# One gate chunk as seven products of 2x2 blocks, in a fused decoder layer on one Trainium2 core

## What is computed

```python
h  = rms_norm(x, mix_norm)
z  = h @ w_in                                  # heads of four mixers, then gl: 4 x 1024 gate columns
o  = stack([o_a, o_b, o_c, o_d], axis=2)       # four branches, 256 wide each
proj = einsum('bsnw,nwd->bsnd', o, w_branch)
gate = sigmoid(gl).reshape(B, S, N_BRANCH, D_MODEL)
merged = sum(gate * proj, axis=2)
x = x + merged @ w_out
x = x + swiglu_ffn(rms_norm(x, ffn_norm), w_gate, w_up, w_down)
```

## Time and profile before

| | us |
|---|---|
| median of 3 runs | 755.29 (755.27 to 755.92) |
| the profiled execution, its own time | 754.7 |
| its span, first to last instruction | 752.9 |
| TensorE busy | 747.9 (99%) |
| VectorE busy | 592.7 (79%) |
| ScalarE busy | 404.8 (54%) |
| GpSimd busy | 104.9 (14%) |

### The profile page before, as it was taken

One profiled execution on the slowest core, in us unless ns is written; L12 is line 12 of the kernel. 1 busy time (PEld: TensorE's weight loads), 2 busy tenths in 40 slices (PEclk: granted clock), 3 DMA queues, 4 the chain that ended last, 5 costly groups with the idle time before them and its releaser, 6 DMA issues.

```text
span 752.9 us, 11500 instructions
## 1 busy us (share of the span) xinstructions
PE 747.9 (99%) x4506; PEld 660.9 (88%) x4506; DVE 592.7 (79%) x819; ACT 404.8 (54%) x629; POOL 104.9 (14%) x131
## 2 busy tenths in 40 slices
PE   8999999999999999999999999999999999999998
PEld 8988888888888888788888899999889999999887
DVE  6655988878788976425978989889989888888991
...
GB/s 292 96 239 56 57 58 112 82 87 57 57 111 112 57 93 75 112 57 279 85 93 169 185 113 167 114 111 199 5 260 110 109 110 109 113 113 328 66 26 84
DMA packets 67877, 89.55 MB, mean 119 GB/s; under 512 B 3108, under 2 KB 52592, under 8 KB 67696
## 3 DMA queue, kind: packets, MB, share of 16 engines
...
q0 software_dynamic: 1456, 3.09, 2.0%
...
## 4 chain that ended last, share of the span: by engine, by line
PE 99%; DVE 0%; issue 0%; POOL 0%; ACT 0%; POOLq 0%; DVEq 0%
PE bank L2365 15%; PE bank L2367 15%; PE bank L2366 15%; PE bank L2795 8%; PE bank L2794 8%; PE bank L2793 8%; PE bank L2874 5%; PE bank L2876 5%; PE bank L2878 5%; PE bank L2732 2%; PE bank L2733 2%; PE bank L2734 2%; PE bank L2764 1%; PE bank L2765 1%; PE bank L2763 1%; PE bank L2580 1%
## 5 line engine op out<-in xcount | busy, mean ns | idle before, releaser
L2365 PE MATMUL bank<-h_hi,w_hi 128*128 128x512 f32 (+1 forms) x352 | 134.7, 383 | 0.0
L2367 PE MATMUL bank<-h_hi,w_lo 128*128 128x512 f32 (+1 forms) x352 | 133.7, 380 | 0.0
L2366 PE MATMUL bank<-h_lo,w_hi 128*128 128x512 f32 (+1 forms) x352 | 133.6, 379 | 0.0
L2793 PE MATMUL bank<-t_hi,w_hi 128*128 128x256 f32 x320 | 88.4, 276 | 0.0
L2795 PE MATMUL bank<-t_hi,w_lo 128*128 128x256 f32 x320 | 88.3, 276 | 0.0
L2794 PE MATMUL bank<-t_lo,w_hi 128*128 128x256 f32 x320 | 88.3, 276 | 0.0
L1538 DVE TENSOR_TENSOR w_lo<-raw,w_hi 128x2048 fp32r<-128x2048 f32 x27 | 64.2, 2381 | 23.4 <-ACT w_hi L927 16.1
L2367 PEld LDWEIGHTS bank<-h_hi,w_lo 128*128 128x128 f32 x352 | 66.2, 188 | 12.7
L2365 PEld LDWEIGHTS bank<-h_hi,w_hi 128*128 128x128 f32 x352 | 66.2, 188 | 12.6 <-issue 0.3
L2366 PEld LDWEIGHTS bank<-h_lo,w_hi 128*128 128x128 f32 x352 | 66.2, 188 | 12.1
L2794 PE MATMUL bank<-f_lo,w_hi 128*128 128x256 f32 x240 | 66.3, 276 | 0.0
...
## 6 DMA issues: line engine op xcount, KB each, us to landing
...
```

Of the source, the lines that this page charges most:

```text
L2365: mm(dst, l_hi, r_hi, start=start, stop=False)
L2366: mm(dst, l_hi, r_lo, start=False, stop=False)
L2367: return mm(dst, l_lo, r_hi, start=False, stop=stop)
L2793: mm(dst, l_hi, r_hi, start=begin and k == 0, stop=False, skip_group_check=True)
```

## The change

The first of the last branch's four gate chunks, chunk 27, gets the kind "seven". It runs as seven block products with `wino_chunk`, 7 x 12 matmuls of 256 columns, in place of 48 matmuls of 512 columns. Its banks are 6 and 7 (the two gate tiles), 2 and 3.

- The sums of h: GpSimd adds high and low parts of four blocks of h back together (`whole_block`, eight instructions of 128x512, between its own adds of the third branch); VectorE makes T3, T1, T2, T4 from them (`gate_sums`, at the end of iteration 24), ScalarE their high parts (iteration 25), VectorE their low parts (`gate_lows`, iteration 25). They lie where the softmax attention's keys and probabilities were.
- The weight sums and low parts: VectorE, four instructions of 128x512 in iteration 24 and four for the low parts at the end of iteration 25; ScalarE four for the high parts, one before each of the first four tiles of chunk 26. The two half splits of chunk 27 fall away on ScalarE and the one split on VectorE.
- ScalarE and VectorE each get a `seven_products` in iteration 27. The two gate tiles are taken after the products: tile 1 after the sixth, tile 0 after the seventh, and in that order they go on to VectorE, GpSimd, `merged_high` and `merged_low`.
- ScalarE's high part of O11 moves from between the two sigmoids of chunk 27 to behind both of them and behind the first `merged_high`. It waits for all seven products as well, since `seven_lo` lies in that memory.
- `out_unit(0)` waits for at least two merged low parts.
- `weight_sums`, `weight_lows`, `wino_split` and `wino_chunk` are moved up in the program so that chunk 27 can call them; the feed-forward part calls them as before, its semaphore counts shifted.

The diff, cut:

```diff
+    SEVEN = MIXER_CHUNKS - D // CW
+    assert chunks[SEVEN][4] == ("gate", N_BRANCH - 1, 0)
+    chunks[SEVEN] = ("seven",) + chunks[SEVEN][1:]
+
+    def gate_tiles(c):
+
+        return (1, 0) if c == SEVEN else (0, 1)
...
+        SEVEN_LO = O11_AT + 3 * LINE // 8
+        seven_lo = place("seven_lo", [P, 7 * QUAD], F32R, at=SEVEN_LO)
+        seven_sum = place("seven_sum", [P, 7 * QUAD], at=SEVEN_LO)
...
+        g_hi = place("g_hi", [P, 4, KT // 2, SEQ // 2], F32R, at=MG0 + 16 * KB)
+        g_lo = place("g_lo", [P, 4, KT // 2, SEQ // 2], F32R, at=MG0)
+        g_sum = place("g_sum", [P, 4, KT // 2, SEQ // 2], at=MG0)
+        g_first = place("g_first", [P, KT // 2, SEQ // 2], at=MG0 + 16 * KB)
...
+        SEVEN_BANK = (bank[6], bank[7], bank[2], bank[3])
...
+            def whole_block(dst, ks, toks):
+
+                for half in range(2):
+                    part = slice(ks.start + 2 * half, ks.start + 2 * half + 2)
+                    ins = pool.tensor_tensor(dst[:, 2 * half:2 * half + 2, :], h_hi[:, part, toks].bitcast(F32),
+                                             h_lo[:, part, toks].bitcast(F32), ALU.add)
+                ins.then_inc(S["t_made"], 1)
+
+            T1, T2, T3, T4 = range(4)
             for m in range(1, N_BRANCH):
-                for d in range(KT):
-                    y = (m - 1) * KT + d
+                for n, d in enumerate(gate_tiles(SEVEN) + tuple(range(CT, KT)) if m == N_BRANCH - 1 else range(KT)):
+                    y = (m - 1) * KT + n
+                    if (m, d) == (N_BRANCH - 2, 4):
+                        pool.wait_ge(S["prob_turned"], HEADS * TT)
+                        whole_block(g_sum[:, T1], LOWER, T2ND)
+                        whole_block(g_sum[:, T2], UPPER, T2ND)
+                    elif (m, d) == (N_BRANCH - 2, 5):
+                        whole_block(g_first, LOWER, T1ST)
+                        whole_block(g_sum[:, T4], UPPER, T1ST)
                     pool.wait_ge(S["gated"], y + 1)
                     if m > 1:
-                        pool.wait_ge(S["proj_added"], y + 1 - KT)
+                        pool.wait_ge(S["proj_added"], (m - 2) * KT + d + 1)
                     pool.tensor_tensor(merged[:, d, :], merged[:, d, :], two[:, y % 2, :], ALU.add)\
                         .then_inc(S["proj_added"], 1)
 
...
-                if d == 0:
+                done = SEVEN_ORDER.index(d)
+                act.wait_ge(S["proj_added"], (N_BRANCH - 2) * KT + done + 1)
+                if done == 0:
                     act.wait_ge(S["attn_out"], 1)
...
                     act.wait_ge(S["o11_in"], 16)
+                    act.wait_ge(S["product_done"], 7)
...
+                    if c + 1 == SEVEN:
+                        if d < 4:
+                            wino_split(SEVEN, (0, 2, 3, 1)[d])
+                    elif d in halves_at:
...
+                    if j == 1 and c == SEVEN - 2:
+                        for i in (2, 0, 1, 3):
+                            act.wait_ge(S["t_made"], SEVEN_SUMS)
+                            nact.activation(g_hi[:, i], g_sum[:, i], ACT.Copy).then_inc(S["t_hi_ready"], 1)
...
+            def seven_products():
+
+                f0, f1, first, last = SEVEN_BANK
+                act.wait_ge(S["product_done"], 1)
+                nact.activation(f0[:, T1ST], first[:, T1ST], ACT.Copy).then_inc(S["c11_seeded"], 1)
+                act.wait_ge(S["product_done"], 2)
+                nact.activation(gate_seventh[:, :], last[:, T1ST], ACT.Copy).then_inc(S["seventh_copied"], 1)
+                act.wait_ge(S["product_done"], 5)
+                nact.activation(f0[:, T2ND], first[:, T1ST], ACT.Copy).then_inc(S["c12_seeded"], 1)
+                for n, j in enumerate(gate_tiles(SEVEN)):
+                    y = (N_BRANCH - 2) * KT + n
+                    if j == 1:
+                        act.wait_ge(S["product_done"], 6)
+                        act.wait_ge(S["c22_ready"], 1)
+                    else:
+                        act.wait_ge(S["product_done"], 7)
+                    act.wait_ge(S["proj_added"], y - 1)
+                    nact.activation(two[:, y % 2, :], SEVEN_BANK[j][:, :], ACT.Sigmoid).then_inc(S["gate_taken"], 1)
+                merged_high(SEVEN_ORDER[0])
+                out_high(O11)
 
...
+                elif c == SEVEN:
+                    seven_products()
...
+            def gate_sums():
+
+                T1, T2, T3, T4 = (g_sum[:, i] for i in range(4))
+                made = SEVEN_SUMS - 4
+                dve.wait_ge(S["t_made"], made)
+                vec.tensor_tensor(T3, T2, T1, ALU.subtract).then_inc(S["t_made"], 1)
+                dve.wait_ge(S["t_made"], made + 1)
+                vec.tensor_tensor(T1, T1, g_first[:, :, :], ALU.subtract).then_inc(S["t_made"], 1)
+                dve.wait_ge(S["t_made"], made + 2)
+                vec.tensor_tensor(T2, T2, T1, ALU.subtract).then_inc(S["t_made"], 1)
+                dve.wait_ge(S["t_made"], made + 3)
+                vec.tensor_tensor(T4, T4, T2, ALU.subtract).then_inc(S["t_made"], 1)
+
+            def gate_lows():
+
+                for n, i in enumerate((2, 0, 1, 3)):
+                    dve.wait_ge(S["t_hi_ready"], n + 1)
+                    vec.tensor_tensor(g_lo[:, i], g_sum[:, i], g_hi[:, i].bitcast(F32), ALU.subtract)\
+                        .then_inc(S["t_lo_ready"], 1)
+
+            def seven_products():
+
+                _, f1, first, _ = SEVEN_BANK
+                dve.wait_ge(S["product_done"], 3)
+                dve.wait_ge(S["seventh_copied"], 1)
+                vec.tensor_tensor(f1[:, T1ST], first[:, T1ST], gate_seventh[:, :], ALU.add).then_inc(S["c21_seeded"], 1)
+                dve.wait_ge(S["product_done"], 6)
+                dve.wait_ge(S["c12_seeded"], 1)
+                vec.tensor_tensor(f1[:, T2ND], first[:, T1ST], gate_seventh[:, :], ALU.add).then_inc(S["c22_ready"], 1)
+
             def gated(c):
 
...
                 _, m, q = chunks[c][4]
-                for j in range(CT):
+                for n, j in enumerate(gate_tiles(c)):
                     d = CT * q + j
-                    y = (m - 1) * KT + d
+                    y = (m - 1) * KT + CT * q + n
                     if q == 0:
                         wait_taken(dve, fill_at[PROJ_AT[m]] + d)
-                    wait_taken(dve, fill_at[c] + j)
+                    if c == SEVEN:
+                        dve.wait_ge(S["gate_taken"], n + 1)
+                    else:
+                        wait_taken(dve, fill_at[c] + j)
                     v = two[:, y % 2, :]
                     vec.tensor_tensor(v, v, branch[:, d, :], ALU.mult).then_inc(S["gated"], 1)
+                    if (c, j) == (SEVEN - 2, 0):
+                        gate_lows()
                     if m == N_BRANCH - 1:
-                        if d > 0:
-                            merged_low(d - 1)
-                        out_behind(d)
+                        if CT * q + n > 0:
+                            merged_low(SEVEN_ORDER[CT * q + n - 1])
+                        out_behind(CT * q + n)
 
             for c in range(MIXER_CHUNKS):
                 kind, _, _, _, what = chunks[c]
...
+                if c == SEVEN - 3:
+                    weight_sums(SEVEN)
+                    gate_sums()
+                elif c == SEVEN - 2:
+                    for step in (0, 2, 3, 1):
+                        weight_lows(SEVEN, step)
...
+                if c == SEVEN:
+                    wino_chunk(c)
                     continue
...
-                        pe.wait_ge(S["mg_lo_ready"], KT // 2 * n + k + 1)
+                        pe.wait_ge(S["mg_lo_ready"], max(KT // 2 * n + k + 1, CT))```

The places that the diff does not show by itself. VectorE around chunk 27, before: the rows from the first gate tile of the last branch to the low part of chunk 29's weights (`o_78`, `o_79`, `o_80` are `o11`, `o12`, `o22`; L1538 is `split`).

```order
L1538 TENSOR_TENSOR w_lo<-raw,w_hi 128x2048 [waits hi_ready] x2
L1913 TENSOR_TENSOR two<-two,branch 128x512 [waits taken1]
L1862 TENSOR_TENSOR o_lo<-o_78,o_hi 128x2048 [waits out_hi]
L1913 TENSOR_TENSOR two<-two,branch 128x512 [waits taken0]
L1855 TENSOR_TENSOR mg_lo<-merged,mg_hi 128x256 [waits mg_hi_ready]
L1867 TENSOR_TENSOR o_79<-o_79,o_78 128x2048 [waits out_t_made,right_half_in]
L1538 TENSOR_TENSOR w_lo<-raw,w_hi 128x2048 [waits hi_ready]
```

280 lines of the change are left out of this document (154 added, 126 removed).

## The result

The changed kernel takes 760.54 us (median of 17 runs, 759.87 to 761.28); the kernel before, beside it on the same chip, takes 755.42. The medians differ by 5.1 us, where 3.8 were forecast. The ratio is 1.0062, with a 95% interval of 1.0051 to 1.0072, which is 4.7 us, between 3.9 and 5.4. Now and then an execution takes some 5 us more than the others of its kernel (two of the 17 of before, 760.4 and 760.85; one of the ten of before beside e1 to e4; two of the twelve of e12), which moves a ratio more than a median. The profiled execution has a span of 758.1 us against 752.9, 5.2 more, with the granted clock of TensorE at 1.00.

A forecast was written before the change was run, and what follows sets the result against it. TensorE, busy 99% of the span, was taken as the bound, with VectorE's queue just under it. Terms -1.36 + 0.1 + 0.35 + 2.25 + 2.0 + 0.45 = +3.8 us gave 759.1 us, range 756.8 to 760.8.

The forecast's parts named there:

- the three late waits: TensorE waits forecast at the head of chunk 29 (2.25 us), in A12 (2.0) and in S2 (0.45).
- the forecast's own upper bound: Whole kernel: 760.0 us in the forecast's own case, if the handovers are longer.
- Chunk 27 is late: Rival, preparing chunk 27: GpSimd's sums slow VectorE, TensorE waits 1 to 3 us more, 761 us; chance 0.08.
- late gates: Chunk 27's gate tiles complete only at its end; VectorE starts O11's low part 5.0 us later.
- signs of being wrong: O11's low part before 355, VectorE idle in chunks 28 to 30, or TensorE waiting at the head of chunk 26 or 27.
- -1.36 forecast for the products: Chunk 27 on TensorE: 48 wide matmuls (10.88 us) replaced by 84 narrow ones (9.52 us), -1.36 us.
- narrow matmuls do not pay: Rival, chunk 27: each 256-column matmul is held to its 188 ns weight load, 760.2 us; chance 0.02.
- The first seed: Third product of chunk 27: ScalarE's seed copy stands behind chunk 28's split, TensorE waits 0.35 us.
- its 4.5 less 0.8: Chunk 29, A12 and S2: the three waits are VectorE's lateness of 4.5 less S2's slack of 0.8.
- only part lands: Rival: chunk 29's wait comes but VectorE makes up for it before the output units, +1.3 us, 756.6; chance 0.10.
- The saving reaches the end: Rival: VectorE's queue gives back 5.0 us or O11 comes by 353, so 753.9 us; chance 0.04.
- All this costs nothing: Preparing chunk 27, iterations 24 and 25: the extra sums and low parts cost zero, upper bound about 1 us.

The follow-up runs named there:

- e1: Kernel before, without seven products, only ScalarE's high part of O11 and its merged high part in chunk 27 as late as the change makes them; ratio to before 1.0047.
- e4: Changed kernel with VectorE's difference o12 - o11 ahead of O11's low part, its wait also counting O22's load; ratio to before 1.0082.
- e12: e10 with the block sums of h back on GpSimd; ratio to before 1.0015, 755.92 us against 755.54 of before.
- e10: Changed kernel with block sums and last branch's adds on VectorE, O11's high part between the sigmoids, chunk 28's weights behind the first seeds; 753.58 us, ratio to before 0.9978.
- e7: Changed kernel with block sums on VectorE, O11's high part between the sigmoids, last gate tile's multiplication first, chunk 28's weights behind the first seeds; ratio to before 1.0014.
- e3: Changed kernel with ScalarE's high part of O11 between the two sigmoids of chunk 27; ratio to before 1.0042.
- e11: Changed kernel with the difference o12 - o11 ahead of O11's low part, waiting for O12's load alone; ratio to before 1.0030.
- e5: Changed kernel with VectorE's multiplication of the last gate tile ahead of OT1's low part and the first two sums for S2; ratio to before 1.0059.
- e2: Changed kernel with the block sums of h made by VectorE as four 1024-column sums, none by GpSimd; ratio to before 1.0052.

## Why the prediction was right, and where it was off

The direction and the three late waits came as forecast, by the mechanism forecast. The number is in the range with some luck: 760.54 is above the forecast's own upper bound, 760.0, and just under the end of the range, 760.8, which had been put near the rival "Chunk 27 is late". What came is what that rival described, the late gates and a wait ahead of them, and one of the prediction's own signs of being wrong, a wait at the head of chunk 26, is there.

*TensorE.* -1.36 forecast for the products. From the head of chunk 27 to that of chunk 28 the time fell from 10.88 to 354.22 - 344.31 = 9.91, which with the wait at the third product is -0.97; forecast -1.01. The narrow matmuls keep their pace of 0.113 us. The rival "narrow matmuls do not pay" is refuted by this and by e10.

*The first seed.* 0.35 forecast, 0.25 measured, and by the cause named: e7 removes it by moving ScalarE's split behind the copy.

*Late gates.* Forecast 2.25 at chunk 29, 2.0 in A12, 0.45 in S2; measured 2.33, 1.73 and 0.32, and some 0.4 us beside them in the longer distances behind these waits. The three are one thing, as the prediction said (its 4.5 less 0.8 is not the sum of the three, which is 4.7, but near what is left of them beside the 1.0 that TensorE gains): e1 makes them without the seven products, and e3 and e11 take 2.2 and 2.4 us out of the sum by two different ways of letting VectorE begin sooner.

*VectorE regains nothing.* The rival "only part lands" asked for idle time in chunks 28 to 30. It is not there: from O11's low part at 358.62 to 395 VectorE stands idle once, for 0.91 us at 391.21, and e5 could gain 0.3 us only.

*The saving reaches the end.* It did not, by this change. e10 shows an arrangement in which it does: O11's low part at 355.00 with the head of chunk 25 at 321.36, which is 354.5 in before's time, and shorter instructions behind it.

*The step that failed: "All this costs nothing".* The preparation of chunk 27 was costed at zero with 1 us as the upper bound; it cost 1.26 us at the head of chunk 26, and e12 against e10 measures GpSimd's block sums alone at 1.27. The walk-through took the four weight sums at 685 ns from a row where GpSimd is idle, and put GpSimd's eight sums at 1.29 each from a row where VectorE is. Side by side they take 1.75 and up to 1.88. The four sums alone came 4 x 1.06 = 4.2 us later to their end, against a slack that the prediction itself had given as 2.8. The rival "Chunk 27 is late" had this mechanism, its row and even its place (chunk 26's weights past 331.88), and its time, 761, is nearer to the 760.5 measured than the forecast's 759.1. It was given 0.08. The Trainium skill says on the page SBUF — State Buffer, section "Who interferes with whom", that a VectorE instruction with two SBUF inputs and a GpSimd instruction that reads SBUF contend; the trace agrees, and e2 shows it. What was wrong was the weight: the mechanism was applied as a rival, though the rows already showed it at work once per gate tile, and every instruction of the preparation was of the kind that it concerns. The walk should have been made with the slowed durations from the start: 4.2 - 2.8 = 1.4 us.

The measured terms add up: -1.36 for the products and 1.26 + 0.25 + 2.33 + 1.73 + 0.32 = 5.89 of waits make 4.53, and the longer distances behind the waits 0.6, so 5.1, against 5.35 from chunk 25 to the end and 5.1 by the medians. Against the forecast's 3.8, the terms that it had (0.1, 0.35, 2.25, 2.0 and 0.45) came out 0.5 smaller; the 1.26 at chunk 26 and the 0.6 of longer distances it did not have.
